# The scaling of the output rows, split anew between the vector, GpSimd and scalar engines

## The reference, cut to what matters

```
    for l in range(DEPTH):
        h = rmsnorm(x, mix_norm[l])
        ...
        x = x + y @ w_out[l]
        h = rmsnorm(x, ffn_norm[l]).reshape(b * s, d)
        x = x + hierarchical_moe(h, ...).reshape(b, s, d)
    return rmsnorm(x, final_norm)

def rmsnorm(x, g):
    x32 = x.astype(jnp.float32)
    y = x32 * lax.rsqrt(jnp.mean(x32 * x32, axis=-1, keepdims=True) + EPS)
    return (y * g.astype(jnp.float32)).astype(x.dtype)
```

## Time and profile before

| | us |
|---|---|
| median of 3 runs | 1972.74 (1972.55 to 1972.74) |
| the profiled execution | 1972.55 |
| its span in the profile | 1970.8 |
| from the last add's end to the span's end | about 14 |

### The profile page before, as it was taken

One profiled execution on the slowest core, in us unless ns is written; L12 is line 12 of the kernel. 1 busy time (PEld: TensorE's weight loads), 2 busy tenths in 40 slices (PEclk: granted clock), 3 DMA queues, 4 the chain that ended last, 5 costly groups with the idle time before them and its releaser, 6 DMA issues.

```text
span 1970.8 us, 21043 instructions
## 1 busy us (share of the span) xinstructions
PE 1826.7 (93%) x9328; PEld 1028.6 (52%) x9328; DVE 602.7 (31%) x833; ACT 183.0 (9%) x290; POOL 260.4 (13%) x107
## 2 busy tenths in 40 slices
PE   8999999999999999989898888899898999889895
PEld 7878888888744444434343443334343443434442
DVE  6212838611231322222231222222232222221224
ACT  4000101111201000000100000000100000000004
POOL 6434544433200000000000000000000000000001
PEclk9999999999999999999999999999999999998998
DMA  9232224444789999999999999999999999999996
GB/s 356 85 102 86 86 87 137 146 172 149 263 348 428 427 429 431 431 430 430 431 429 430 431 431 430 429 431 430 430 430 430 431 430 430 431 430 430 430 429 257
DMA packets 68024, 684.01 MB, mean 347 GB/s; under 512 B 10629, under 2 KB 11269, under 8 KB 40585
## 3 DMA queue, kind: packets, MB, share of 16 engines
q1 hardware_dynamic: 65096, 674.84, 82.4%
q0 software_dynamic: 2304, 8.39, 1.1%
q10 hardware_dynamic: 576, 0.14, 0.0%
HBM read 683.35 MB, written 8.39 MB: 351 GB/s over the span
## 4 chain that ended last, share of the span: by engine, by line
PE 64%; DMA 32%; DVE 1%; SPq 1%; ACT 0%; issue 0%; DVEq 0%; ACTq 0%
PE banks L1252 21%; DMA region_h<-in_w_gate 16%; DMA region_h<-in_w_up 14%; PE banks L882 12%; PE banks L1272 10%; PE banks L1053 9%; PE banks L1190 4%; PE banks L878 2%; PE banks L1175 2%; DMA region_h<-in_w_down 1%; DMA region_rest<-in_w_in 1%; PE banks L1164 1%; PE banks L1225 1%; PE banks L1263 1%; DVE region_w L1766 1%
## 5 line engine op out<-in xcount | busy, mean ns | idle before, releaser
L1252 PE MATMUL banks<-region_rest,region_w 128*64 128x384 f32 x2048 | 347.1, 493 | 41.7 <-DMA region_rest<-in_w_gate 41.0
L1740 DVE TENSOR_TENSOR region_x<-banks,region_x 128x1024 f32<-128x1024 f32 x120 | 141.3, 1219 | 580.4 <-PE banks L1190 580.4
L1272 PE MATMUL banks<-region_rest,region_w 128*64 128x512 f32 x1080 | 270.7, 657 | 28.3 <-DVE region_w L1766 20.6
L1252 PEld LDWEIGHTS banks<-region_rest,region_w 128*64 128x64 f32 x2048 | 143.5, 138 | 240.4 <-issue 168.7
L546 POOL TENSOR_TENSOR split_w<-region_rest,split_w 128x2048 fp32r<-128x2048 f32 x42 | 197.7, 4707 | 268.2 <-DVE split_w L1404 268.0
L882 PE MATMUL banks<-split_h,split_w 128*128 128x512 f32 x736 | 230.3, 392 | 0.8 <-DVE split_w L1397 0.5
L1252 PE MATMUL banks<-region_h,region_w 128*64 128x384 f32 x1024 | 173.7, 492 | 44.1 <-DMA region_h<-in_w_gate 24.4
L1272 PEld LDWEIGHTS banks<-region_rest,region_w 128*64 128x64 f32 x1080 | 81.3, 151 | 197.8 <-issue 168.0
L607 POOL DMA_INDIRECT region_h<-x_rows,region_rest x16 | 16.0, 1002 | 1246.3 <-PE banks L1175 1242.8
L1252 PE MATMUL banks<-region_w 128*64 128x384 f32 x1024 | 172.1, 489 | 0.4 <-DMA region_w<-in_w_up 0.4
L1053 PE MATMUL banks<-split_w,split_h 128*128 128x512 f32 x512 | 159.1, 392 | 0.0
(11 more groups left out here) (244 smaller groups left out, 1251.8 us busy)
## 6 DMA issues: line engine op xcount, KB each, us to landing
region_rest<-in_w_down SPq DMA_DIRECT2D x45, 3072.0 KB, 29.3
region_rest<-in_w_gate SPq DMA_DIRECT2D x33, 3072.0 KB, 23.6
region_rest<-in_w_up SPq DMA_DIRECT2D x30, 3072.0 KB, 23.8
region_w<-in_w_up SPq DMA_DIRECT2D x17, 3072.0 KB, 30.7
region_h<-in_w_gate SPq DMA_DIRECT2D x16, 3072.0 KB, 23.7
region_h<-in_w_up SPq DMA_DIRECT2D x15, 3072.0 KB, 22.8
region_h<-in_w_down SPq DMA_DIRECT2D x15, 3072.0 KB, 24.0
region_w<-in_w_gate SPq DMA_DIRECT2D x14, 3072.0 KB, 32.2
```

Of the source, the lines that this page charges most:

```text
L1252: mm = t_.matmul(ps[h * SLOTS:(h + 1) * SLOTS, u, 0:HF], hTe[:, k, :], ring_gu[slot][:, kk, h * HF:(h + 1) * HF], start=(k == 0), stop=(k ...
L1272: mm = t_.matmul(ps[g * SLOTS:(g + 1) * SLOTS, 6 + n, :], aT[:, kk, q * SLOTS:(q + 1) * SLOTS], ring_down[slot][:, kk, (2 * c + n) * 512:( ...
L1740: v.tensor_tensor(tile, ps[:, 2 + 2 * c:4 + 2 * c, :], tile, ALU.add).then_inc(comb_added, 1)
```

## The change

FINAL becomes 1024, so DVE's instruction covers 1024 columns in place of 1280, and the first half of each tile goes by way of `gained`. POOL's four multiplications get 1024 columns in place of 768. The scaling of that half is now done by POOL itself for tiles 0 and 1 (a new instruction on it, `tensor_scalar` with the reciprocal as a number for each partition), and by ACT for tiles 2 and 3 alone, with a semaphore of its own, `last_rest_ready`. SP waits for the one or the other. ACT's calls are put in another order: the early squares of tile 2 first, then the four `rms_last`, then its two scalings.

```
-FINAL = 768
+FINAL = D // 2
...
             for t in range(NT):
                 pool.wait_ge(last_added, added(0, t))
                 g.tensor_tensor(gained[:, t, :], x_sb[:, t, 0:FINAL], final_row[:, 0:FINAL], ALU.mult).then_inc(f_gained, 1)
+            for t in range(NT // 2):
+                pool.wait_ge(f_rinv, t + 1)
+                pool.wait_ge(f_gained, t + 1)
+                g.tensor_scalar(x_sb[:, t, 0:FINAL], gained[:, t, :], stat[:, 8 + t:9 + t], None, ALU.mult)\
+                    .then_inc(out_rest_ready, 1)
...
-            rms_last(0)
             ae.wait_ge(last_added, added(0, 2))
             square_first(2, f_pre, 5)
-            rms_last(1)
-            scale_rest(0)
-            rms_last(2)
-            scale_rest(1)
-            rms_last(3)
-            scale_rest(2)
-            scale_rest(3)
+            for t in range(NT):
+                rms_last(t)
+            for t in range(NT // 2, NT):
+                scale_rest(t)
```

More of the change, by code:

```diff
@@ L300, in build @@
         tile_used = sem("tile_used")
+        last_rest_ready = sem("last_rest_ready")
         half_used, half_landed = sem("half_used"), sem("half_landed")
@@ L515, in _ @@
                     sp.wait_ge(out_ready, t + 1)
-                    sp.wait_ge(out_rest_ready, t + 1)
+                    if t < NT // 2:
+                        sp.wait_ge(out_rest_ready, t + 1)
+                    else:
+                        sp.wait_ge(last_rest_ready, t + 1 - NT // 2)
                     sp.dma_start(out_v[:, t, :], x_sb[:, t, :]).then_inc(out_saved, 16)
@@ L855, in scale_rest @@
                 ae.wait_ge(f_rinv, t + 1)
-                a.activation(x_sb[:, t, 0:FINAL], gained[:, t, :], ACT.Copy, scale=stat[:, 8 + t:9 + t]).then_inc(out_rest_ready, 1)
-            rms_last(0)
+                a.activation(x_sb[:, t, 0:FINAL], gained[:, t, :], ACT.Copy, scale=stat[:, 8 + t:9 + t]).then_inc(last_rest_ready, 1)
             ae.wait_ge(last_added, added(0, 2))
             square_first(2, f_pre, 5)
-            rms_last(1)
-            scale_rest(0)
-            rms_last(2)
-            scale_rest(1)
-            rms_last(3)
-            scale_rest(2)
-            scale_rest(3)
+            for t in range(NT):
+                rms_last(t)
+            for t in range(NT // 2, NT):
+                scale_rest(t)
         @block.tensor
```

## The result

| | median us | runs |
|---|---|---|
| before, beside the changed kernel | 1974.36 | 22 (1971.80 to 1976.74) |
| changed | 1977.45 | 22 (1974.86 to 1979.51) |

The ratio is 1.0014 with a 95% interval of 1.0009 to 1.0020. The changed kernel is slower by 0.14%, some 2.8 us (0.0014 x 1974.36; by the interval 1.8 to 3.9 us), less than the 0.2% that was taken as the bound for a difference.

What follows compares the result with a forecast made beforehand. The prediction took the output stream's start plus 10.6 us, plus any gap, as the bound. A 0.27 us earlier start and a 0.39 us gap made +0.12 us on the 1972.74 median: 1972.9 us, range 1972.0 to 1975.7.

Steps and rivals of the forecast that it cites:

- a stream that never runs dry: Output transfer at the kernel's end: said to flow without gaps for 10.6 us at 395 GB/s, setting the end.
- X: Duration of one new POOL scaling of 1024 columns: taken as 1.04 us, kept between 0.95 and 2.39.
- the price of two operands: Rival on POOL's scalings: each costs as much as a two-operand product, 2.39 us, giving 1975.5; chance 16%.
- POOL much slower: Rival on POOL's scalings ahead of tile 1's issue: over 3.9 us slower from 2.95 us each, 1977.8 at 3.5; 4%.
- The turns: POOL and DVE scalings on SBUF: each blocks the other, DVE first, delaying tile 1 and opening a 0.39 us gap.
- 1967.84 + 2X: Formula for the end: two POOL scalings of duration X lie in line up to tile 1's issue.
- 0.82 + 7.95: After tile 1's issue: 0.82 us until bytes flow, then 7.95 us of stream to the end.
- buys nothing: ACT's chain through tile 3's root: said not to set the end, so its 3.1 us earlier root gains nothing.
- 0.27 us is all that can be won: DVE's shorter tile 0 scaling starts the output 0.27 us sooner; claimed as the change's whole possible gain.
- ACT's order is worth nothing by itself: ACT's reordered squares, roots and scalings: said only to keep ACT out of the way, with no gain alone.
- the forecast's mechanism at 60%: Main case at the output: POOL and DVE take turns with a cheap POOL scaling, giving 1972.9; chance 60%.
- no change: Whole kernel time: difference said to stay within 0.2%, that is 3.9 us; chance 94%.

Runs made afterwards that it cites:

- psum_operand: Changed kernel, but DVE's four scalings take their weights from PSUM instead of SBUF; last adds to span's end 19.89 us (changed 21.63).
- copy_cost: Changed kernel, but POOL's two scalings are plain copies, leaving those columns unscaled; last adds to span's end 19.44 us (changed 21.63).
- tt_bcast: Changed kernel, but POOL scales by a product with the reciprocal spread over the row; last adds to span's end 20.35 us (changed 21.63).
- size_only: Kernel before with 1024 for 768 columns, ACT doing all four scalings in its old order; last adds to span's end 19.46 us (before 18.72).
- act_all: Kernel before with 1024 columns, all scalings on ACT, roots of tiles 0 to 2 ahead of their scalings; last adds to span's end 18.57 us (before 18.72).

## Why the prediction was wrong

**What bounds the kernel: right, but for one hole.** A tail of first issue, stream and holes accounts for all ten kernels of the table. But "a stream that never runs dry" was read off an average over 10.6 us, and 0.4 us of these were a hole. The first issue came where it was forecast, 0.27 us sooner (6.03 against 6.30), DVE's 1.28 us for 1024 columns was exact, and ACT's root of tile 3 was done at 1963.81, which is 1959.82 on the clock of the kernel before (forecast 1959.81). The stream ran at 403 GB/s.

**The step that failed: X, the price of POOL's scaling.** Taken as 1.04 us with bounds of 0.95 and 2.39, it is 2.85. The value was scaled up from a copy of 8 columns and a select of 128, and the upper bound rested on the thought that an operation with one operand can't cost more than one with two. The copy's price was right to a hundredth (1.03), but a scaling isn't a copy: on this engine it costs more than a product. The row nearest by operands was not nearest by operation. The truth lies between two rivals: "the price of two operands" (X = 2.39, 16%) and "POOL much slower" (from X = 2.95 on, 4%). The first has the measured +2.8 us to the digit, by luck: its price is 0.46 us too low, and two other terms made up for it. The second has the mechanism, a scaling dearer than a two-operand product.

**The turns: right that they exist, wrong in size and order.** The 5.11 us of the earlier trace rows did mean contention, and psum_operand shows it directly: 1.74 us of the loss. By the forecast's own formula, 1967.84 + 2X, a price of 2.85 would have given 1973.54, +3.7 us; +2.9 were measured. Half of the difference, 0.44 us, lies in the turns: the formula has tile 1 issued at 1964.77, measured it is 1964.33 on the clock of the kernel before. DVE behind this operation was blocked for 0.67 us, not to POOL's end, so it was done with tile 1 before POOL was done with tile 0, and POOL's second scaling waited only 0.6 us, for DVE's tile 2 (3.45 us against 2.85). The other 0.39 us lie behind tile 1's issue: 9.38 us to the end of the span, where the forecast's 0.82 + 7.95 and the 1.0 us after the stream make 9.77, with the hole of the kernel before counted as transfer. The forecast carried over the turns of one kind of POOL instruction to another. It took the engine whose record starts first to have the first turn; that was right in the changed kernel, but in copy_cost and tt_bcast it was the other.

**A check left out.** The forecast compared the issues of tiles 1 and 3 with what the stream needs, but not tile 2's. There the kernel before already had a hole of 0.4 us, behind ACT's root of tile 3, and size_only lost 0.74 us through it. So it doesn't hold that time off ACT's chain "buys nothing", nor that 0.27 us is all that can be won. That ACT's order is worth nothing by itself fails too, given the new size: act_all's order was worth 0.89 us against size_only. What the order of the change itself is worth wasn't run by itself; in the changed kernel POOL's holes cover it.

**The number.** Forecast 1972.9, range 1972.0 to 1975.7, measured 1977.45. Against the 22 runs of the kernel before, +0.12 was forecast, at most about +3.0, and the ratio says +2.8. So as a difference the result just lies inside the range, thanks to the upper bound on X and to the two terms above that were too long, and not to the forecast's mechanism at 60%. The absolute range was missed by the level as well: its base was three runs that lay 1.6 us below the median of 22. The forecast of no difference of more than 0.2% stands; within it the sign "no change" doesn't, since the interval excludes 1.

## What to carry to other kernels

Where a kernel ends with a stream of output, find when it starts and lay each later issue against what the stream needs by then, every one of them, and read the stream in stretches of a few tenths of a us, since an average over all of it hides a hole. An engine's work costs nothing until it opens a hole, and costs all of it afterwards. An operation that the trace doesn't show on an engine is not bounded by one with more operands; take its price from the same operation or measure it. And a second engine beside one that reads two operands from SBUF is not a second engine's worth of work: here the helper's instruction cost the main engine 0.67 us (scaling), 0.86 (copy of 1.03) or 1.74 (product of 1.89).

## What the runs showed of the hardware

- On POOL, 1024 float32 columns: copy 1.03 us, product with a spread number 1.89, product of two tiles 2.34, scaling by a constant 2.77, scaling by a number for each partition 2.85.
- DVE with two SBUF operands behind a POOL copy or product waits to its end (2.14 and 3.02 us for an instruction of 1.28, ending 1.08 us after POOL's in both); behind a POOL `tensor_scalar` it waited only 0.67 us (1.95). With one of DVE's operands in PSUM neither waits. The Trainium skill ("SBUF — State Buffer", section "SBUF: two separate sides") has the shared port pair held for the whole instruction by whichever starts first: the copy and the product agree. The 1.95 us doesn't: DVE ended 0.66 us before the POOL instruction that had started ahead of it. Why was not tried.
- Which engine gets the first turn can't be read from the starts of the records: with DVE's record 0.03 us (copy) and 0.05 us (product) ahead of POOL's, POOL went first; with DVE's 0.06 us ahead (scaling), DVE did.
- The output's 4.19 MB take 10.2 us of transfer without a hole. The bytes flow 0.8 us after the first issue (1959.2 after 1958.38 in the kernel before), and the span ends 1.0 to 1.6 us after the stream's last full stretch.
